# The second feed-forward of a two-layer block: another order of its seven-block products, and one low part moved from VectorE to GpSimd

## The chip, the core and the metric

The kernel runs on one core of a Trainium2 chip. The metric is device time in microseconds (us) of one execution, the median of several. The engines are named as in the profile: PE is TensorE (matmuls), PEld its weight loads, DVE is VectorE, ACT is ScalarE, POOL is GpSimd, SP is SyncE, which issues the DMAs here.

## What is computed

The program computes two model blocks of 1024 tokens by 1024 channels in float32. The change touches only the last stage, the feed-forward of the second block:

```python
h = rms_norm(x, norm_mlp[l])
x = x + jnp.square(jax.nn.relu(h @ w_up[l])) @ w_down[l]     # 1024 -> 4096 -> 1024
return rms_norm(x, norm_final)
```

## The kernel before

A float32 product is made of three matmuls of a faster format: every operand is split in a high part (a cast on ACT) and a low part (value minus high part), and the three are high by high, high by low and low by high. The `high` casts of weights are at L334 (ACT), the `low` subtractions of weights at L340 (POOL).

`square_ffn` cuts the 4096 hidden channels into 16 chunks of 256 (`chunks`). For a chunk the upward product (`up(i)`) and the downward product (`down(i)`) are each seen as a product of 2 by 2 blocks and made with seven block products instead of eight (the Strassen-Winograd scheme), named P1 to P7. The price is sums: of weight blocks (POOL, `pair_low` and `row_low`), of the activations' blocks (DVE, `first_blocks`, L2241 to L2246), of the upward results (DVE, `combine`, L2226 to L2235). Each of the seven products is 12 matmuls of 128x512, so a chunk is 168 matmuls. The program is pipelined by one chunk: `up(i)` and then `down(i)` run on PE, and `down(i)` takes the activations that `up(i - 1)` made. Chunk 16's rows of the downward product are done plainly at the end (`last_tile`), followed by the final norm. So PE does `up(0)`, `up(1)`, `down(1)`, then 14 times `up(i)`, `down(i)` for i = 2 to 15, then the last tiles.

The steps that the change touches:

- **The ring of weights** (`TurnRing`): a chunk has 14 split weight blocks, places 0 to 6 for `up`, 7 to 13 for `down`, in seven slots. A place can be written when the product seven places back has been taken (`used`). `split` counts finished low parts. The raw tiles (two, `core.raw`) hold by turns the chunk's two tiles of `w_up` and its two rows of `w_down`. `load_up` (SP) loads the next chunk's two `w_up` tiles once the low parts 12 and 13 are made. `weigh` (POOL, L396) multiplies each `w_up` tile by the norm's gain.
- **DVE's order in a chunk**: the low parts of the activation blocks P1, P2, P4 (`a_low`, L2220), sums, P5's low part, sums; `combine`; then `take` for the seven downward products in the order P1 P2 P5 P4 P6 P7 P3, with the low parts of P6, P7 and P3 between them. A `take` is four adds (L2256) of one PSUM bank each into X. PE writes the four banks in turn and needs a bank's add done before it writes that bank for the next product.
- **ACT's order in a chunk**, `fall(i - 1)` and then `rise(i)`:

```python
def fall(i, following):
    a_high(i, "P6")
    following(0)            # high(i + 1, 0): waits for weigh on POOL
    a_high(i, "P7")
    relu_first(i)
    a_high(i, "P3")
    following(1)
    relu_second(i)
    for n in range(2, 6):
        following(n)
```

`rise(i)` is `high(i, 6)`, `a_high(i, "P1", "P2", "P4", "P5")`, `keep(i)` (a copy of the first upward result, L2129, without which PE may not start the fifth upward product) and the seven casts of `w_down` blocks. Each engine works strictly in its written order; the waits are semaphores.
- **Start and end**: the second chunk's `w_up` tiles lie in a place of their own and POOL weighs them. Two differences in X (L2213, L2214) are made first of all on DVE, their sums (L2280, L2281) at the end, after the low parts of chunk 16 (L2278).

Of the kernel before, what the change touches and what calls it, by code (L numbers as in the profile page):

```python
# [23 lines left out]
P = 128  # L24
# [409 lines left out]
class TurnRing(Ring):  # L434


    UP, DOWN_PRODUCTS = 7, ("P1", "P2", "P5", "P4", "P6", "P7", "P3")
# [43 lines left out]
    def load_last(self, sp, i, sources):  # L481

        for n, p in enumerate((12, 13)):
# [20 lines left out]
    def row_low(self, pool, i):  # L504
# [11 lines left out]
        self.low(pool, i, 9, self.S)  # L516
        pool.wait_ge(self.split, self.done(i, 9))
# [451 lines left out]
class Program:  # L969
# [997 lines left out]
    def square_ffn(self, name, ring, W_up, W_down, rows):  # L1967
# [5 lines left out]
        MADE = ("P1", "P2", "P4", "P5", "P6", "P7", "P3")  # L1973
        PLACE = {"P1": 0, "P2": 1, "P4": 2, "P5": 3, "P6": 0, "P7": 1, "P3": 3}
        with ExitStack() as ctx:
# [6 lines left out]
                "kept", "u6", "u5", "u7", "c21", "c12", "relu", "sq", "a_sum", "a_hi", "a_lo", "down_mm", "down_add")}  # L1982
# [9 lines left out]
            ring.give_second([self.at(f"{name}_second_raw{k}", [P, UNIT], base + at * UNIT) for k, at in enumerate((8, 12))],  # L1992
# [20 lines left out]

            @block.sync
            def _(sp):
# [12 lines left out]
                sp.wait_ge(ring.used, ring.done(chunks - 1, 10))  # L2028
# [7 lines left out]
            def _(pool):  # L2036
# [16 lines left out]
            def _(pe):  # L2053
                def up(i):
                    X, Z, W, Y = up_banks(i)
                    out = {"P1": X, "P2": X, "P5": W, "P4": W, "P7": Z, "P3": Z, "P6": Y}
                    for n, product_name in enumerate(PRODUCTS):
                        more = product_name in ("P2", "P3", "P4")
                        if product_name == "P1" and not (isinstance(i, int) and i < 2):
                            pe.wait_ge(s["relu"], i * 3 - 2)  # L2060
                        elif product_name == "P5" and not (isinstance(i, int) and i < 2):
                            pe.wait_ge(s["relu"], i * 3 - 1)
# [18 lines left out]
                def down(i):  # L2081
                    for n, product_name in enumerate(DOWNS):
                        more = product_name in ("P2", "P3", "P4")
                        pe.wait_ge(ring.split, ring.done(i, 7 + n))
                        pe.wait_ge(s["a_lo"], made(i, MADE.index(product_name) + 1))
# [25 lines left out]
                pe.wait_ge(s["a_lo"], made(chunks, 2))  # L2111
# [6 lines left out]
            def _(act):  # L2118
# [12 lines left out]
                def relu_first(i):  # L2131
# [5 lines left out]
                    act.wait_ge(s["relu"], i * 3 + 1)  # L2137
                    act.activation(U[0], U[0], ACT.Square).then_inc(s["sq"], 1)

                def relu_second(i):  # L2140

                    if not (isinstance(i, int) and i == 0):
                        act.wait_ge(s["a_lo"], made(i, 7))
                    act.activation(A12, up_banks(i)[2], ACT.Relu).then_inc(s["relu"], 1)
                    act.activation(u22, u22, ACT.Relu).then_inc(s["relu"], 1)
                    act.wait_ge(s["relu"], i * 3 + 3)
                    act.activation(U[1], U[1], ACT.Square).then_inc(s["sq"], 1)

                def a_high(i, *names):

                    for x in names:
                        if x in ("P1", "P2", "P4"):
                            act.wait_ge(s["sq"], i * 2 - (1 if x == "P1" else 0))
                            if not (isinstance(i, int) and i == 1):
                                act.wait_ge(ring.used, ring.done(i - 1, 7 + DOWNS.index({"P1": "P6", "P2": "P7", "P4": "P4"}[x])))
                            else:
# [961 lines left out]
```

## Time and profile before

| | us |
|---|---|
| median of 3 runs | 2860.82 (2858.64 to 2862.8) |
| the profiled execution | 2861.63, its span 2859.9 |
| PE busy in the span | 2724.5 (95%) |
| DVE busy | 1750.1 (61%) |
| POOL busy | 1754.1 (61%) |
| ACT busy | 1129.4 (39%) |

The stage of the change is the last 680 us of the span. Busy shares are averages over all stages. A matmul's time in the rows is its own from start to end (about 0.39 us); since matmuls overlap, the distance between two starts is what one costs.

### The profile page before, as it was taken

What the parts mean: (1) busy time and instruction counts of PE and PEld (TensorE: products, weight loads), DVE (VectorE), ACT (ScalarE), POOL (GpSimd) and SP (SyncE); (2) the same over time, 40 slices, a digit from 0 to 9 for tenths busy, and PEclk for the clock granted to TensorE, in tenths of its full rate; (3) what the DMA queues carried; (4) which work ended last, traced back from release to release, by engine and by line L of the source; (5) the groups of instructions that cost most, each with busy time, mean ns of one, the idle gap of its engine ahead of it and who ended that gap; (6) DMA issues with size and microseconds to landing.
All of it is one profiled execution on the core that took longest, in us unless ns stands there. A gap on an engine that the chain in (4) does not pass through costs nothing. (4 is left out here: it accounts for less than half of the span.)

```text
span 2859.9 us, 39241 instructions
## 1 busy us (share of the span) xinstructions
PE 2724.5 (95%) x13371; PEld 2246.3 (79%) x13371; DVE 1750.1 (61%) x2209; ACT 1129.4 (39%) x1684; POOL 1754.1 (61%) x1201
## 2 busy tenths in 40 slices
PE   8999998999999999799999999999998999999998
PEld 7888886888888887678778878878786777777776
DVE  5334435565555656575685685685535877777778
ACT  4312316333332334555355345445333433443443
POOL 3323336767777676765565565565337787777782
PEclk9999999999999999899999999999999999999999
DMA  3111111111212113212111111112601111111112
GB/s 121 45 38 37 45 38 30 45 44 51 59 46 64 44 51 96 66 34 60 49 49 60 49 48 59 49 48 59 221 15 44 45 44 59 44 44 59 44 47 92
DMA packets 196117, 160.28 MB, mean 56 GB/s; under 512 B 5719, under 2 KB 176300, under 8 KB 196013
## 3 DMA queue, kind: packets, MB, share of 16 engines
q1 hardware_dynamic: 196013, 158.83, 18.1%
q8 instruction: 73, 1.20, 0.2%
q14 instruction: 31, 0.25, 0.0%
HBM read 143.08 MB, written 15.73 MB: 56 GB/s over the span
## 5 line engine op out<-in xcount | busy, mean ns | idle before, releaser
L340 POOL TENSOR_TENSOR w_lo<-w_raw,w_hi 128x512 fp32r<-128x512 f32 x336 | 466.2, 1395 | 316.9 <-ACT w_hi L334 316.9
L334 ACT CAST w_hi<-w_raw 128x512 fp32r<-128x512 f32 x336 | 202.8, 617 | 432.3 <-DMA w_raw<-in_w_in 106.2
L546 PE MATMUL PA<-h_hi,w_hi 128*128 128x512 f32 x636 | 260.7, 410 | 17.7 <-PEq L1035 5.6
L548 PE MATMUL PA<-h_hi,w_lo 128*128 128x512 f32 x636 | 250.0, 393 | 0.0
L547 PE MATMUL PA<-h_lo,w_hi 128*128 128x512 f32 x636 | 249.7, 393 | 0.0
L340 POOL TENSOR_TENSOR w_lo<-f_sums,w_hi 128x512 fp32r<-128x512 f32 x128 | 201.8, 1577 | 10.5 <-ACT w_hi L334 10.5
L396 POOL TENSOR_TENSOR w_raw<-w_raw,params 128x1024 f32<-128x1024 f32 x72 | 137.2, 1918 | 90.1 <-DMA w_raw<-in_w_up 45.5
L340 POOL TENSOR_TENSOR w_lo<-hy_ring_sums,w_hi 128x512 fp32r<-128x512 f32 x96 | 140.4, 1463 | 61.6 <-ACT w_hi L334 61.6
L546 PE MATMUL PB<-f_t_hi,w_hi 128*128 128x512 f32 x424 | 169.4, 400 | 8.5 <-ACT hy_tm L2797 5.0
L547 PE MATMUL PB<-f_t_lo,w_hi 128*128 128x512 f32 x424 | 166.3, 392 | 0.0
L548 PE MATMUL PB<-f_t_hi,w_lo 128*128 128x512 f32 x424 | 166.3, 392 | 0.0
L546 PEld LDWEIGHTS PA<-h_hi,w_hi 128*128 128x128 f32 x636 | 120.8, 190 | 47.8 <-issue 13.5
L2220 DVE TENSOR_TENSOR f_a_lo<-f_u,f_a_hi 128x512 fp32r<-128x512 f32 x105 | 122.4, 1188 | 58.1 <-ACT f_a_hi L2164 58.1
L125 POOL TENSOR_TENSOR w_hi<-w_raw,params 128x1024 fp32r<-128x1024 f32 x24 | 45.5, 1895 | 169.2 <-PE PB L136 82.8
L547 PEld LDWEIGHTS PA<-h_lo,w_hi 128*128 128x128 f32 x636 | 120.8, 190 | 27.3 <-issue 3.8
L548 PEld LDWEIGHTS PA<-h_hi,w_lo 128*128 128x128 f32 x636 | 120.5, 189 | 26.0
L2256 DVE TENSOR_TENSOR X<-X,MM 128x512 f32<-128x512 f32 x210 | 137.4, 680 | 0.2 <-PE MM L2093 0.2
L2256 DVE TENSOR_TENSOR X<-X,DD 128x512 f32<-128x512 f32 x210 | 136.8, 680 | 0.4 <-PE DD L2093 0.4
L409 POOL TENSOR_TENSOR hy_ring_sums<-w_raw 128x512 f32<-128x512 f32 x32 | 45.2, 1412 | 120.4 <-DMA w_raw<-in_w_in 120.4
L2091 PE MATMUL DD<-w_hi,f_a_hi 128*128 128x512 f32 x180 | 75.0, 416 | 43.6 <-DVE X L2256 43.6
L334 ACT CAST w_hi<-hy_ring_sums 128x512 fp32r<-128x512 f32 x96 | 59.6, 621 | 143.0 <-POOL hy_ring_sums L409 68.8
L334 ACT CAST w_hi<-f_sums 128x512 fp32r<-128x512 f32 x128 | 79.3, 619 | 79.5 <-POOL f_sums L421 35.8
(664 smaller groups left out, 8273.2 us busy)
## 6 DMA issues: line engine op xcount, KB each, us to landing
w_raw<-in_w_in SPq DMA_DIRECT2D x64, 512.0 KB, 5.2
w_raw<-in_ffn_w_up SPq DMA_DIRECT2D x42, 512.0 KB, 4.7
w_raw<-in_w_down SPq DMA_DIRECT2D x32, 512.0 KB, 3.7
w_raw<-in_w_up SPq DMA_DIRECT2D x30, 512.0 KB, 4.7
w_raw<-in_gla_w_in SPq DMA_DIRECT2D x24, 512.0 KB, 3.7
w_lo_raw<-in_ffn_w_down SPq DMA_DIRECT2D x44, 256.0 KB, 2.6
X<-in_x SPq DMA_DIRECT2D x8, 512.0 KB, 7.8
w_raw<-in_gla_w_out SPq DMA_DIRECT2D x8, 512.0 KB, 3.6
```

The lines of the kernel that those rows point to most:

```text
L125: pool.tensor_tensor(hi, raw, self.core.zero[:, 0:1].broadcast_to([P, UNIT]), ALU.add)\
L334: act.copy(self.slot(i, p)[0], source).then_inc(self.hi_done, 1)
L340: pool.tensor_tensor(lo, source, hi.bitcast(F32), ALU.subtract).then_inc(self.split, 1)
L396: pool.tensor_tensor(raw, raw, column.unsqueeze(2).broadcast_to([P, KT, P]), ALU.mult)\
L409: pool.tensor_tensor(self.S, a21, a22, ALU.add).then_inc(self.summed, 1)
L546: pe.matmul(bank, ah[:, k, :], bh[:, k, :], start=(k == 0 and not more), stop=False, skip_group_check=more)
L547: pe.matmul(bank, ah[:, k, :], bl[:, k, :], start=False, stop=False, skip_group_check=more)
L548: mm = pe.matmul(bank, al[:, k, :], bh[:, k, :], start=False, stop=(k == 3), skip_group_check=more)
L2091: pe.matmul(bank(b), hi[:, tok], wh, start=not more, stop=False, skip_group_check=more)
L2220: dve.tensor_tensor(alo[k], BLOCK[x], ahi[k].bitcast(F32), ALU.subtract).then_inc(s["a_lo"], 1)
L2256: dve.tensor_tensor(rows_, rows_, bank(b), op).then_inc(s["down_add"], 1)
```

## The change

Only the second feed-forward changes. The downward products run in the order P1 P2 P7 P3 P5 P4 P6 (before P1 P2 P5 P4 P6 P7 P3); the activation blocks are split in the order P4 P1 P2 P7 P3 P5 P6. The low part of P3's block is made by POOL, at the end of its chunk, and no longer by DVE. ACT casts all blocks before it starts the next chunk's weights; both relus of the second pair come before those of the first. The kept result lies in A21 and no longer in A22. The next chunk's `w_up` tiles are loaded after the low parts 9 and 12. ACT, not POOL, weighs the second chunk's tiles, with 16 multiplications of 128x128. The two differences in X come after `combine(0)`, and the low parts of chunk 16 before the last `take`.

```diff
-    UP, DOWN_PRODUCTS = 7, ("P1", "P2", "P5", "P4", "P6", "P7", "P3")
+    UP, DOWN_PRODUCTS = 7, ("P1", "P2", "P7", "P3", "P5", "P4", "P6")
@@ load_up, load_last
-        for n, p in enumerate((12, 13)):
+        for n, p in enumerate((9, 12)):
@@ row_low (POOL)
         pool.tensor_tensor(b12, b12, b22, ALU.subtract).then_inc(self.mixed, 1)
-        self.low(pool, i, 9, self.S)
-        pool.wait_ge(self.split, self.done(i, 9))
+        pool.wait_ge(self.mixed, first + 2)
+        self.low(pool, i, 9, b12)
+        self.low(pool, i, 10, b22)
+        self.low(pool, i, 11, self.S)
+        pool.wait_ge(self.split, self.done(i, 11))
         pool.tensor_tensor(self.S, b22, self.S, ALU.add).then_inc(self.mixed, 1)
         pool.wait_ge(self.mixed, first + 3)
         pool.tensor_tensor(b21, b21, self.S, ALU.subtract).then_inc(self.mixed, 1)
-        self.low(pool, i, 10, b21)
-        self.low(pool, i, 11, self.S)
-        self.low(pool, i, 12, b12)
-        self.low(pool, i, 13, b22)
+        pool.wait_ge(self.mixed, first + 4)
+        self.low(pool, i, 12, b21)
+        self.low(pool, i, 13, self.S)
@@ square_ffn
-        MADE = ("P1", "P2", "P4", "P5", "P6", "P7", "P3")
-        PLACE = {"P1": 0, "P2": 1, "P4": 2, "P5": 3, "P6": 0, "P7": 1, "P3": 3}
+        MADE = ("P4", "P1", "P2", "P7", "P3", "P5", "P6")
+        LATE = ('P3',)
+        EARLY = tuple(x for x in MADE if x not in LATE)
+        PLACE = {"P1": 0, "P4": 1, "P2": 2, "P7": 3, "P3": 0, "P5": 2, "P6": 3}
...
-            u22 = A22
+            u22 = A21
@@ POOL, chunk(i)
-                    ring.weigh(pool, i)
+                    if not (isinstance(i, int) and i == 1):
+                        ring.weigh(pool, i)
                     for part in range(2):
                         ring.pair_low(pool, i, 0, i, part)
                     ring.row_low(pool, i)
+                    for x in LATE:
+                        k = PLACE[x]
+                        pool.wait_ge(s["a_hi"], made(i, MADE.index(x) + 1))
+                        pool.tensor_tensor(alo[k], BLOCK[x], ahi[k].bitcast(F32), ALU.subtract)\
+                            .then_inc(s["a_lo_late"], 1)
@@ PE, up(i)
                         if product_name == "P1" and not (isinstance(i, int) and i < 2):
-                            pe.wait_ge(s["relu"], i * 3 - 2)
-                        elif product_name == "P5" and not (isinstance(i, int) and i < 2):
-                            pe.wait_ge(s["relu"], i * 3 - 1)
+                            pe.wait_ge(s["relu"], i * 3)
@@ ACT
                 def keep(i):
                     act.wait_ge(ring.used, ring.done(i, 0))
                     if not (isinstance(i, int) and i == 0):
-                        act.wait_ge(s["a_sum"], i * 4 - 1)
-                        act.wait_ge(s["a_lo"], made(i, 4))
+                        act.wait_ge(*low_done(i, "P7"))
...
+                def relu_second(i):
                     act.wait_ge(s["c12"], i + 1)
                     if not (isinstance(i, int) and i == 0):
-                        act.wait_ge(s["a_lo"], made(i, 6))
+                        act.wait_ge(*low_done(i, "P3"))
+                        act.wait_ge(*low_done(i, "P5"))
...
                 def rise(i):
+                    a_high(i, "P4", "P1", "P2")
                     high(i, 6)
-                    a_high(i, "P1", "P2", "P4", "P5")
+                    a_high(i, "P7")
                     keep(i)
...
                 def fall(i, following):
-                    a_high(i, "P6")
+                    a_high(i, "P3", "P5", "P6")
+                    relu_second(i)
                     following(0)
-                    a_high(i, "P7")
                     relu_first(i)
-                    a_high(i, "P3")
-                    following(1)
-                    relu_second(i)
-                    for n in range(2, 6):
+                    for n in range(1, 6):
                         following(n)
...
+                def weigh_second():
+                    for n in range(2):
+                        raw = ring.raw(1)[n].rearrange("p (k n) -> p k n", k=KT)
+                        act.wait_ge(*ring.arrived(n, 1))
+                        for k in range(KT):
+                            scaled = act.mul(raw[:, k, :], raw[:, k, :], c.par[:, ring.column + k:ring.column + k + 1])
+                        scaled.then_inc(ring.weighted, 1)
@@ ACT, the start
                 keep(0)
+                weigh_second()
                 high(0, 6)
-                high(1, 0, 1, 2, 3, 4)
+                high(1, 0, 1, 2, 3)
+                relu_second(0)
                 relu_first(0)
-                relu_second(0)
-                high(1, 5)
+                high(1, 4, 5)
                 rise(1)
@@ DVE
-                    for x in ("P1", "P2", "P4"):
+                    for x in ("P4", "P1", "P2"):
                         a_low(i, x)
                     dve.tensor_tensor(A22, A21, A22, ALU.add).then_inc(s["a_sum"], 1)
                     dve.tensor_tensor(A21, A11, A21, ALU.subtract).then_inc(s["a_sum"], 1)
-                    a_low(i, "P5")
+                    dve.wait_ge(s["a_sum"], i * 4 - 3)
                     dve.tensor_tensor(A11, A22, A11, ALU.subtract).then_inc(s["a_sum"], 1)
+                    a_low(i, "P7")
...
                     take(i, "P1")
                     take(i, "P2")
+                    a_low(i, "P5")
+                    take(i, "P7")
                     a_low(i, "P6")
+                    take(i, "P3")
                     take(i, "P5")
-                    a_low(i, "P7")
                     take(i, "P4")
-                    a_low(i, "P3")
+                    if isinstance(i, int) and i == chunks - 1:
+                        last_lows()
                     take(i, "P6")
-                    take(i, "P7")
-                    take(i, "P3")
...
                 combine(0)
+                dve.tensor_tensor(X12, X12, X22, ALU.subtract)
+                dve.tensor_tensor(X21, X21, X22, ALU.subtract)
                 chunk(1)
```

## Rows read from the trace of the kernel before

**Rows 1.** Busy time by stretch: chunk 1, and chunks 2 to 15

```profile
core 0: us, PE busy (x) PEld busy (x) DVE busy (x) ACT busy (x) POOL busy (x), PEclk, DMA share, GB/s
2180.50:2229.60 49.10, 40.62 (x168) 32.52 (x167) 30.20 (x44) 22.76 (x36) 38.35 (x30) 0.93 0.08 22
2229.60:2823.50 593.90, 552.45 (x2355) 448.83 (x2353) 457.58 (x618) 229.59 (x378) 453.75 (x331) 0.98 0.16 50
```

**Rows 2.** Waits from 2050 to 2860 us: total, times, longest

```profile
ACT w_hi L334 <- POOL w_raw L396: 94.6, 14, 7.2
...
PE DD L2091 <- DVE X L2256: 43.6, 22, 3.6
```

**Rows 3.** Timeline of PE: start, duration, work [idle before it, until whom]

```profile
2229.95 0.39 PE L2073 MATMUL PA<-h_hi,w_hi 128*128 128x512 f32 x1
...
2263.62 0.64 PE L2091 MATMUL DD<-w_hi,f_a_hi 128*128 128x512 f32 x1 [3.59 <-DVE X L2256]
2264.06 0.63 PE L2092 MATMUL DD<-w_lo,f_a_hi 128*128 128x512 f32 x1
...
2391.46 0.50 PE L2091 MATMUL DD<-w_hi,f_a_hi 128*128 128x512 f32 x1 [2.59 <-DVE X L2256]
2395.66 0.50 PE L2091 MATMUL DD<-w_hi,f_a_hi 128*128 128x512 f32 x1 [1.18 <-DVE X L2256]
...
2401.23 0.39 PE L2073 MATMUL PA<-h_hi,w_hi 128*128 128x512 f32 x1
...
2420.27 0.39 PE L2091 MATMUL DD<-w_hi,f_a_hi 128*128 128x512 f32 x1
...
2823.09 0.39 PE L2093 MATMUL MM<-f_seventh_hi,f_a_lo 128*128 128x512 f32 x1
```

**Rows 4.** Timeline of ACT in the chunk that starts at 2401.23

```profile
2402.42 1.66 ACT L2164 CAST f_a_hi<-f_u 128x512 fp32r<-128x512 f32 x3
...
2411.00 0.59 ACT L2129 COPY f_u<-PA 128x512 f32<-128x512 f32 x1 [1.44 <-DVE f_u L2244]
...
2430.93 0.62 ACT L334 CAST w_hi<-w_raw 128x512 fp32r<-128x512 f32 x1 [7.12 <-POOL w_raw L396]
```

**Rows 5.** Timeline of DVE around the same chunk

```profile
2393.50 1.51 DVE L2220 TENSOR_TENSOR f_a_lo<-f_u,f_a_hi 128x512 fp32r<-128x512 f32 x1 [0.30 <-ACT f_a_hi L2164]
...
2403.06 4.08 DVE L2220 TENSOR_TENSOR f_a_lo<-f_u,f_a_hi 128x512 fp32r<-128x512 f32 x3 [0.88 <-ACT f_a_hi L2164]
...
2426.52 0.69 DVE L2220 TENSOR_TENSOR f_a_lo<-f_u,f_a_hi 128x512 fp32r<-128x512 f32 x1
2427.12 1.28 DVE L2256 TENSOR_TENSOR X<-X,DD 128x512 f32<-128x512 f32 x2
2428.31 1.28 DVE L2256 TENSOR_TENSOR X<-X,MM 128x512 f32<-128x512 f32 x2
2432.10 1.40 DVE L2220 TENSOR_TENSOR f_a_lo<-f_u,f_a_hi 128x512 fp32r<-128x512 f32 x1 [2.51 <-ACT f_a_hi L2164]
```

**Rows 6.** Timeline of POOL in the same chunk

```profile
2404.25 1.74 POOL L340 TENSOR_TENSOR f_seventh_lo<-f_sums,f_seventh_hi 128x512 fp32r<-128x512 f32 x1
...
2412.19 2.56 POOL L340 TENSOR_TENSOR w_lo<-w_raw,w_hi 128x512 fp32r<-128x512 f32 x2 [3.90 <-ACT w_hi L334]
...
2420.78 1.30 POOL L340 TENSOR_TENSOR w_lo<-w_raw,w_hi 128x512 fp32r<-128x512 f32 x1 [0.80 <-ACT w_hi L334]
...
2424.55 1.29 POOL L340 TENSOR_TENSOR f_seventh_lo<-w_raw,f_seventh_hi 128x512 fp32r<-128x512 f32 x1
2428.92 1.91 POOL L396 TENSOR_TENSOR w_raw<-w_raw,params 128x1024 f32<-128x1024 f32 x1 [3.07 <-DMA w_raw<-in_w_up]
```

**Rows 7.** Timeline of PE in chunk 1 and at the end

```profile
2180.38 0.39 PE L2073 MATMUL PA<-h_hi,w_hi 128*128 128x512 f32 x1
...
2197.69 0.79 PE L2073 MATMUL PA<-h_hi,w_hi 128*128 128x512 f32 x1 [6.27 <-ACT f_u L2129]
...
2826.59 0.50 PE L134 MATMUL DD<-w_hi,h_hi 128*128 128x512 f32 x1 [3.11 <-DVE h_lo L2278]
```

More of the change, by code:

```diff
@@ L481, in load_last @@
     def load_last(self, sp, i, sources):
-        for n, p in enumerate((12, 13)):
+        for n, p in enumerate((9, 12)):
             sp.wait_ge(self.split, self.done(i - 1, p))
@@ L1981, in square_ffn @@
             s = {n: self.sem(f"{name}_{n}") for n in (
-                "kept", "u6", "u5", "u7", "c21", "c12", "relu", "sq", "a_sum", "a_hi", "a_lo", "down_mm", "down_add")}
+                "kept", "u6", "u5", "u7", "c21", "c12", "relu", "sq", "a_sum", "a_hi", "a_lo", "a_lo_late", "down_mm", "down_add")}
             adds = 28 * (chunks - 1)
@@ L2027, in _ @@
                 ring.load_last(sp, chunks, rows_of(chunks))
-                sp.wait_ge(ring.used, ring.done(chunks - 1, 10))
+                sp.wait_ge(ring.used, ring.done(chunks - 1, 11))
                 sp.dma_start(row, rows[0].partition_broadcast(P)).then_inc(fin.row_in, 16)
@@ L2084, in down @@
                         pe.wait_ge(ring.split, ring.done(i, 7 + n))
-                        pe.wait_ge(s["a_lo"], made(i, MADE.index(product_name) + 1))
+                        pe.wait_ge(*low_done(i, product_name))
                         hi, lo = ahi[PLACE[product_name]], alo[PLACE[product_name]]
@@ L2110, in _ @@
                     down(i)
-                pe.wait_ge(s["a_lo"], made(chunks, 2))
+                pe.wait_ge(s["a_lo"], len(EARLY) * (chunks - 1) + 2)
                 pe.wait_ge(ring.split, ring.done(chunks, 3))
@@ L2136, in relu_first @@
+                def relu_first(i):
+                    if not (isinstance(i, int) and i == 0):
+                        act.wait_ge(*low_done(i, "P6"))
                     act.activation(U[0], pair_of(i)[0], ACT.Relu).then_inc(s["relu"], 1)
-                    act.wait_ge(s["relu"], i * 3 + 1)
+                    act.wait_ge(s["relu"], i * 3 + 3)
                     act.activation(U[0], U[0], ACT.Square).then_inc(s["sq"], 1)
[L2140 to L2147, printed above, removed]
+                SLOT_BEFORE = {"P1": (1, "P3"), "P4": (1, "P4"), "P2": (1, "P5"), "P7": (1, "P6"),
+                               "P3": (0, "P1"), "P5": (0, "P2"), "P6": (0, "P7")}
@@ L2149, in a_high @@
+                SUM = {"P5": 1, "P7": 2, "P6": 3, "P3": 4}
                 def a_high(i, *names):
                     for x in names:
[L2152 to L2156, printed above, removed]
-                                act.wait_ge(ring.split, ring.done(1, 5))
-                        else:
-                            act.wait_ge(s["a_sum"], i * 4 - {"P5": 3, "P7": 2, "P6": 1, "P3": 0}[x])
-                            if x != "P5":
-                                act.wait_ge(ring.used, ring.done(i, 7 + DOWNS.index({"P6": "P1", "P7": "P2", "P3": "P5"}[x])))
-                            elif not (isinstance(i, int) and i == 1):
-                                act.wait_ge(ring.used, ring.done(i - 1, 13))
+                        if x in SUM:
+                            act.wait_ge(s["a_sum"], i * 4 - 4 + SUM[x])
+                        else:
+                            act.wait_ge(s["sq"], i * 2 - (0 if x == "P1" else 1))
+                        back, taker = SLOT_BEFORE[x]
+                        if not (isinstance(i, int) and i == 1 and back):
+                            act.wait_ge(ring.used, ring.done(i - back, 7 + DOWNS.index(taker)))
+                        elif x in ("P2", "P7"):
+                            act.wait_ge(ring.split, ring.done(1, 5 if x == "P2" else 4))
@@ L2256, in take, with last_lows @@
                         dve.tensor_tensor(rows_, rows_, bank(b), op).then_inc(s["down_add"], 1)
+                def last_lows():
+                    for k in (1, 0):
+                        dve.wait_ge(s["a_hi"], made(chunks, 2 - k))
+                        dve.tensor_tensor(last_lo[k], U[k], last_hi[k].bitcast(F32), ALU.subtract).then_inc(s["a_lo"], 1)
                 def chunk(i):
@@ L2262, in chunk @@
                     take(i, "P2")
+                    a_low(i, "P5")
+                    take(i, "P7")
                     a_low(i, "P6")
+                    take(i, "P3")
                     take(i, "P5")
-                    a_low(i, "P7")
                     take(i, "P4")
-                    a_low(i, "P3")
+                    if isinstance(i, int) and i == chunks - 1:
+                        last_lows()
                     take(i, "P6")
-                    take(i, "P7")
-                    take(i, "P3")
                 combine(0)
+                dve.tensor_tensor(X12, X12, X22, ALU.subtract)
+                dve.tensor_tensor(X21, X21, X22, ALU.subtract)
                 chunk(1)
-                with dve.Fori(2, chunks) as i:
+                with dve.Fori(2, chunks - 1) as i:
                     chunk(i)
-                for k in range(2):
-                    dve.wait_ge(s["a_hi"], made(chunks, k + 1))
-                    dve.tensor_tensor(last_lo[k], U[k], last_hi[k].bitcast(F32), ALU.subtract).then_inc(s["a_lo"], 1)
+                chunk(chunks - 1)
                 dve.wait_ge(s["down_add"], adds + 1)
```

17 lines of the change are left out of this document (11 added, 6 removed).

## The prediction

> **What bounds the kernel now.** I read the busy time by stretch first, then the waits, then the timelines of the four engines over one chunk. The page says that PE is busy 95% of the span, so only what PE waits for can be won. From the first matmul of `up(2)` at 2229.95 to the start of the last one of `down(15)` at 2823.09, 0.23 before its slot ends, PE takes 593.4 us for 14 chunks, 42.4 each [rows 3]. What a chunk would cost without waits comes from one upward half: 84 matmuls between 2401.23 and 2420.27, that is 19.04 us, or 0.227 a matmul [rows 3]; a chunk has 168, so 38.1. Each chunk loses 4.3 us.
>
> The waits say where: PE's four-bank products (L2091) stood 43.6 us behind DVE's adds into X [rows 2]. The timeline shows two forms. In one, PE waits 2.59 and, 4 us later, 1.18. In the other it waits once, up to 3.59, and the next matmuls then start 0.43 apart (2263.62, 2264.06) and not 0.23: the clock stands at its lower level for about nine of them, which costs 1.8 us [rows 3]. Both forms cost about 4.
>
> Why DVE is late is on its own timeline: after P5's take it stood idle 2.51 before P7's low part at 2432.10, until ACT's high part came [rows 5]. ACT had nothing to do for 7.12 until 2430.93, because the cast written ahead of P7's needs the next chunk's `w_up` tile weighed by POOL [rows 4]. That is the wait of 94.6 us over 14 chunks [rows 2]. POOL in turn waited 3.07 for a DMA that could start only when low part 12 was done (the low part 13 starts at 2424.55, the tile is there at 2428.92) [rows 6]. So the chain is DMA, weighing, ACT's order, DVE, PE. The second wait of 1.18 is a low part of 1.51 that DVE had to make when it was already as late as PE bears [rows 3, 5].
>
> **The change in a chunk.** Let t be the time since the first matmul of `up(i)`; the downward products start at 19.0, 21.8, 24.5, 27.2, 29.9, 32.6 and 35.4.
>
> *ACT's order.* `fall` now casts P3, P5 and P6 before anything that needs the next chunk. P5's slot is free at 24.5 (P2 done), its high part there at 25.1; DVE ends P2's take then too. P6's is there at 27.9, before DVE asks. The wait of 2.5 is gone. What takes its place: `following(0)` now stands behind `relu_second`, which needs P5's low part (26.6) and P3's from POOL, and `relu_first` behind P6's (about 30.5). With 2.1 for relu and square the relus end near 33; PE now wants all three before `up(i + 1)`, at 39. Six us of cover; nothing charged.
>
> *DVE between takes.* Three low parts become two. An add costs 0.60 when DVE runs behind (pairs at 2427.12 and 2428.31, 1.19 apart [rows 5]), PE makes a bank in 0.68, so DVE gains 0.32 a product, and it may be 3 x 0.68 - 0.60 = 1.4 late before PE stands. A low part is 0.69 when POOL is idle and 1.40 to 1.51 beside POOL's work [rows 5]; POOL will be at work, so I take 1.4. P5's uses the 1.4 up, P7's take gives 0.3 back, P6's 1.4 then costs PE 1.0. The trace's own price for this is 1.18 with a wait of 0.30 in it, 0.9 [rows 3, 5]. Bounds: 0.1 if both are quick, 1.7 if both last 1.74 like the slowed neighbour on POOL [rows 6]. The term is 1.0: a chunk of 39.1. One wait of this length left the matmul spacing at 0.23 (2395.66), so no clock is lost [rows 3].
>
> *DVE's first blocks.* They began at 2403.06, 0.88 late, for ACT's casts at 2402.42 stood behind a weight cast [rows 4, 5]. Those casts now come first. So P7's low part, and `keep` after it, come near t = 9.2 to 9.8 where `keep` was at 9.8 (2411.00) [rows 4]. PE needs it at 10.9: no wait, 0.5 to 1.1 of cover.
>
> *POOL.* It worked 453.75 / 14 = 32.4 us a chunk [rows 1]. P3's low part adds 1.3 (its 128x512 neighbours, 2.56 for two) to 1.74 [rows 6]; I take 1.4. Its new order also puts a wait for ACT's cast ahead of low part 9, as the one of 0.80 at 2420.78 [rows 6]. Walked: low part 7 starts 1.2 after `keep` starts (2412.19 after 2411.00), at 10.4 to 11.0; from there to the end of low part 13 it was 13.65 (2425.84), now 14.45; P3's ends 1.4 later, at t = 26.3 to 26.9 [rows 4, 6]. PE takes it at 27.2. The cover is thin, 0.3 to 0.9, and I charge nothing. All in all POOL has 32.4 + 1.4 + 0.8 for the new wait + 0.5 for more meetings with DVE = 35.1 of work and forced waiting, then the 0.8 that stays, 0.9 for the row DMA and about 1.3 between dependent sums: 38.1, one under PE's 39.1.
>
> *SP's queue.* The tiles are asked for after low parts 9 and 12, the second at t = 24, and need 4.4 (2428.92 less 2424.55) [rows 6], so 28.4; POOL has low part 13, P3's and the first weighing (1.91) until then. At most 0.5 idle, inside POOL's slack.
>
> **Chunk 1.** It lasts from 2180.38 to 2229.95, 49.6, 11.5 over the floor: PE waited 6.27 for `keep` and then ran at the lower clock [rows 3, 7]. POOL no longer weighs (2 x 1.91 [rows 6]). ACT does it in 16 pieces between two casts; for a 128x128 piece the trace has no row, and from its 128x512 casts of 0.62 [rows 4] each lies between a quarter, 0.16, and 0.62: 2.5 to 10 us, and I take 0.3 each, 4.8, which ends before POOL's next sum. But the two differences in X now lie on DVE ahead of the low parts, and P2's high part waits for a raw tile to be used up. I put `keep` 2.6 earlier, 2.5 more from a shorter spell of low clock and the downward waits: 5, bounds 0 (10 us of multiplications) and 8.
>
> **The end.** PE waited 3.11 for the low parts of chunk 16 and then lost about 1.8 in clock [rows 7]. They now lie before the last take, so PE stands about 1.2 there, and later about 1.5 because X's two sums keep DVE from the first adds. Saved: 4.9 - 2.7 = 2.2.
>
> **Sum.** 14 x (42.4 - 39.1) = 46, + 5 + 2 = 53. The profiled execution took 2861.6; 2861.6 - 53 = 2808.6. It lies 0.8 above the median of the runs, so 2808.
>
> The Trainium skill ("SBUF — State Buffer", "Who interferes with whom") says that a VectorE instruction with two SBUF inputs and a GpSimd instruction that reads SBUF exclude each other for the whole instruction, and "Perfetto Trace Analysis" ("Optimizing Scalar/DVE Operations") warns that moving work between the two might not help. The rows of 1.40 beside 0.69 agree, and the adds out of PSUM, at 1.28 a pair, show nothing of it. If every POOL operation and every such DVE operation of a chunk stood in one line, the result would be the third rival's.
>
> **The rivals.**
>
> *POOL sets the pace (24%).* If `keep` comes 1 us later or POOL's operations meet DVE more often, P3's low part ends after 27.2 and PE waits there, and DVE's lateness is partly made up meanwhile. For: cover of only 0.3 to 0.9. Against: POOL's own sum is 38.1. At 40.5 a chunk: 14 x 1.9 + 5 + 2 = 34 saved, 2827.
>
> *DVE's low parts stay hidden (14%).* One or both fall into POOL's idle time (0.69). Then 38.3 a chunk: 57 + 5 + 2 = 64, 2797.
>
> *The two engines exclude each other, and time is lost (9%).* This one ends on the other side. Its place is POOL's chain from low part 7 to P3's low part. It decides once that part ends after t = 27.2 + 4.3 + 0.5 = 32: from there the new wait of PE is longer than the old ones and the gain of start and end. For that each of POOL's 23 operations of 128x512 in a chunk must take 1.74 [rows 6] in place of 1.3, adding 10 us: 48 a chunk, 14 x 5.7 - 7 = 73 lost, 2934. Half of them would give 43, about the time before. Against it: beside DVE's three low parts in a row, 4.08 together, POOL lost only 0.45 once [rows 5, 6].
>
> *The reorder does nothing (3%),* because PE's wait has another releaser: 2861. The idle 2.51 and 7.12 speak against it.
>
> **How the numbers follow.** The forecast has 50%, its own range 2802 to 2817 (chunks of 38.7 to 39.7). The range of 2794 to 2833 takes in both neighbours and leaves out the last two. A measurement of this kernel can tell about 0.2% (6 us) from no change. Faster: 50 + 24 + 14 and a little of the third, 0.89; same 0.04; slower 0.07.
>
> **What would show it.** On the changed profile: a chunk of 39.1 on PE, with one wait of about 1.0 before the fifth downward product and none over 2; matmul spacing of 0.23 all through; ACT's `f_a_hi` waiting for PE and no longer behind `w_raw` L396; POOL's new low part on L340's sibling line at t = 26 to 27; PE's wait at 2197.69 shorter; no wait of 3.11 at the end. The prediction is wrong if PE waits before the fourth downward product (POOL), or before the fifth upward one (`keep`).

## The result

The changed kernel takes 2824.28 us (median of 4 runs, 2824.13 to 2824.3) against 2859.73 for the kernel before in the same session. The ratio is 0.9876 with a 95% interval of 0.9858 to 0.9893: 35.5 us won. The prediction was 2808 with a range of 2794 to 2833: the direction and the range held, the gain was forecast at 53, half as much again. The profiled execution has a span of 2822.4.

Busy time by stretch in the changed kernel, for chunk 1, chunks 2 to 15 and the end (the columns are those of [rows 1]):

```profile
2177.50:2225.00 47.50, 41.17 (x170) 33.01 (x169) 38.76 (x45) 23.22 (x37) 39.30 (x27) 0.93 0.08 23
2225.00:2788.00 563.00, 542.21 (x2353) 438.09 (x2351) 467.61 (x602) 229.78 (x375) 489.68 (x345) 1.00 0.18 53
2788.00:2822.40 34.40, 22.68 (x98) 17.86 (x96) 29.07 (x47) 10.06 (x24) 0.00 (x0) 0.91 0.31 123
```

From the first matmul of `up(2)` at 2224.90 to the end of `down(15)`'s last slot at 2788.19 the 14 chunks take 563.3 us, 40.2 each, where it was 42.4: 38.7 for the first and about 40.4 for those behind it. PE's granted clock is 1.00 in them, where it was 0.98. GpSimd works 35.0 us a chunk (489.68 / 14), where it was 32.4 [rows 1]. The timeline of PE shows the new waits of one chunk:

```profile
2424.88 0.39 PE L2107 MATMUL MM<-f_seventh_hi,f_a_lo 128*128 128x512 f32 x1
2425.11 0.39 PE L2087 MATMUL PA<-h_hi,w_hi 128*128 128x512 f32 x1
...
2437.42 0.49 PE L2087 MATMUL PA<-h_hi,w_hi 128*128 128x512 f32 x1 [1.27 <-ACT f_u L2142]
...
2454.31 0.49 PE L2105 MATMUL DD<-w_hi,f_a_hi 128*128 128x512 f32 x1 [0.29 <-DVE X L2278]
```

The waits of 2.59 and 1.18 [rows 3] are gone. In their place PE waits 1.3 before the fifth upward product, for ACT's copy (`keep`), and 0.3 before the fourth downward one, P3's (three products of 2.72 after 2445.70). From start to start these cost about 1.5 and 0.7 in the chunk shown, which takes 40.3; over the 14 chunks, of which the first has neither, it is about 1.5 and 0.6, and with 38.1 that is the 40.2. The second wait is named after DVE's add, but that add had ended at about 2453.5, as the pair that began at 2452.84 shows, and GpSimd's low part of P3 only at 2454.0:

```profile
2452.84 1.27 DVE L2278 TENSOR_TENSOR X<-X,DD 128x512 f32<-128x512 f32 x2
```

```profile
2452.33 1.74 POOL L2059 TENSOR_TENSOR f_a_lo<-f_u,f_a_hi 128x512 fp32r<-128x512 f32 x1
2454.03 4.21 POOL L396 TENSOR_TENSOR w_raw<-w_raw,params 128x1024 f32<-128x1024 f32 x2
```

In the run below without that low part this wait is absent. Why the copy is late is on DVE and ACT. DVE's first blocks, then ACT's casts ahead of them:

```profile
2424.63 1.37 DVE L2278 TENSOR_TENSOR X<-X,MM 128x512 f32<-128x512 f32 x2
2426.82 4.14 DVE L2241 TENSOR_TENSOR f_a_lo<-f_u,f_a_hi 128x512 fp32r<-128x512 f32 x3 [0.83 <-ACT f_a_hi L2179]
2430.89 1.78 DVE L2262 TENSOR_TENSOR f_u<-f_u,f_u 128x512 f32<-128x512 f32 x1
2432.59 1.77 DVE L2263 TENSOR_TENSOR f_u<-f_u 128x512 f32<-128x512 f32 x1
2434.28 1.79 DVE L2265 TENSOR_TENSOR f_u<-f_u,f_u 128x512 f32<-128x512 f32 x1
2436.00 0.68 DVE L2241 TENSOR_TENSOR f_a_lo<-f_u,f_a_hi 128x512 fp32r<-128x512 f32 x1
```

```profile
2424.61 0.62 ACT L334 CAST w_hi<-f_sums 128x512 fp32r<-128x512 f32 x1 [2.00 <-POOL f_sums L421]
2425.14 1.14 ACT L334 CAST w_hi<-w_raw 128x512 fp32r<-128x512 f32 x2
2426.18 1.66 ACT L2179 CAST f_a_hi<-f_u 128x512 fp32r<-128x512 f32 x3
...
2436.71 0.58 ACT L2142 COPY f_u<-PA 128x512 f32<-128x512 f32 x1 [1.62 <-DVE f_a_lo L2241]
```

Two things are to be seen. DVE's three sums take 1.78 each; in the trace of before one of them did and two took 0.68. (The third takes 1.78 in 7 of the 14 chunks; in the chunk before this one it took 0.68, and P7's low part behind it 1.54 in its place.) And DVE still stands 0.83 before its first low part, because the casts of the activation blocks are written behind three weight casts, of which the first waits for GpSimd's third sum. The copy of the chunk before is on ACT at 2396.34:

```profile
2396.34 0.58 ACT L2142 COPY f_u<-PA 128x512 f32<-128x512 f32 x1 [1.60 <-DVE f_a_lo L2241]
```

The timeline of POOL from there on shows that it now works beside DVE's second and third sum (2432.08 and 2434.24), where it had stood idle for 3.90 [rows 6]:

```profile
2397.52 2.55 POOL L340 TENSOR_TENSOR w_lo<-w_raw,w_hi 128x512 fp32r<-128x512 f32 x2 [1.76 <-ACT w_hi L334]
...
2411.96 1.76 POOL L2059 TENSOR_TENSOR f_a_lo<-f_u,f_a_hi 128x512 fp32r<-128x512 f32 x1
2413.68 4.21 POOL L396 TENSOR_TENSOR w_raw<-w_raw,params 128x1024 f32<-128x1024 f32 x2
2418.07 1.30 POOL L409 TENSOR_TENSOR f_sums<-w_raw 128x512 f32<-128x512 f32 x1 [0.18 <-POOL w_raw L396]
...
2423.21 1.29 POOL L421 TENSOR_TENSOR f_sums<-f_sums,w_raw 128x512 f32<-128x512 f32 x1
...
2428.68 3.43 POOL L340 TENSOR_TENSOR w_lo<-w_raw,w_hi 128x512 fp32r<-128x512 f32 x2
2432.08 1.73 POOL L340 TENSOR_TENSOR f_seventh_lo<-f_sums,f_seventh_hi 128x512 fp32r<-128x512 f32 x1
2434.24 1.29 POOL L510 TENSOR_TENSOR f_sums<-w_raw 128x512 f32<-128x512 f32 x1 [0.43 <-DMA w_raw<-in_w_down]
```

Read from one copy (2396.34) to the next (2436.71), the chain closes on itself: 1.2 to low part 7, 14.4 to P3's low part (2411.96), 1.7 for it, 4.4 for the two weighings, 6.4 to the end of the third sum, 2.3 through ACT's casts, 4.1 for three low parts on DVE, 5.1 for its three sums, 0.7 for P7's low part: 40.4. This loop is longer than PE's 38.1, so PE waits in every chunk but the first. The theory that the runs led to is this loop (L), with the meetings of DVE and GpSimd in it (M: the two make each other's operations longer). The rivals were that the meetings alone count, that GpSimd's chain alone is the pace (P), and that ACT's order alone was the whole gain. The expectations of the first four runs go by M and its rivals; L was put on record only after them.

### The profile page after: what moved, and what is told of

Same layout as the page of the kernel before. It is cut to its first block and busy times, and to the rows that moved or that the text cites. A ratio compares the mean times of both kernels' runs of the same rounds, so it can differ in the third digit from the quotient of the medians.

```text
span 2822.4 us, 39258 instructions
## 1 busy us (share of the span) xinstructions
PE 2713.2 (96%) x13371; PEld 2235.3 (79%) x13371; DVE 1765.8 (63%) x2194; ACT 1136.1 (40%) x1700; POOL 1785.2 (63%) x1214
## 5 line engine op out<-in xcount | busy, mean ns | idle before, releaser
L340 POOL TENSOR_TENSOR w_lo<-w_raw,w_hi 128x512 fp32r<-128x512 f32 x351 | 495.3, 1420 | 293.9 <-ACT w_hi L334 293.9
L334 ACT CAST w_hi<-w_raw 128x512 fp32r<-128x512 f32 x351 | 209.7, 617 | 388.8 <-DMA w_raw<-in_w_in 121.2
L340 POOL TENSOR_TENSOR w_lo<-f_sums,w_hi 128x512 fp32r<-128x512 f32 x113 | 174.0, 1540 | 10.7 <-ACT w_hi L334 10.7
L548 PEld LDWEIGHTS PA<-h_hi,w_hi 128*128 128x128 f32 x636 | 120.9, 190 | 47.9 <-issue 13.7
L409 POOL TENSOR_TENSOR hy_ring_sums<-w_raw 128x512 f32<-128x512 f32 x32 | 44.3, 1385 | 121.5 <-DMA w_raw<-in_w_in 121.5
L2241 DVE TENSOR_TENSOR f_a_lo<-f_u,f_a_hi 128x512 fp32r<-128x512 f32 x90 | 110.6, 1254 | 12.9 <-ACT f_a_hi L2179 12.9
L334 ACT CAST w_hi<-hy_ring_sums 128x512 fp32r<-128x512 f32 x96 | 59.6, 621 | 139.5 <-POOL hy_ring_sums L409 68.2
L334 ACT CAST w_hi<-f_sums 128x512 fp32r<-128x512 f32 x113 | 70.2, 621 | 111.8 <-POOL f_sums L421 60.9
L2179 ACT CAST f_a_hi<-f_u 128x512 fp32r<-128x512 f32 x105 | 62.2, 619 | 119.5 <-DVE f_u L2263 74.7
```

The lines of the kernel that those rows point to most:

```text
L334: act.copy(self.slot(i, p)[0], source).then_inc(self.hi_done, 1)
L340: pool.tensor_tensor(lo, source, hi.bitcast(F32), ALU.subtract).then_inc(self.split, 1)
L409: pool.tensor_tensor(self.S, a21, a22, ALU.add).then_inc(self.summed, 1)
L548: pe.matmul(bank, ah[:, k, :], bh[:, k, :], start=(k == 0 and not more), stop=False, skip_group_check=more)
L2179: act.copy(ahi[PLACE[x]], BLOCK[x]).then_inc(s["a_hi"], 1)
L2241: dve.tensor_tensor(alo[k], BLOCK[x], ahi[k].bitcast(F32), ALU.subtract).then_inc(s["a_lo"], 1)
```

## The experiments

Twelve kernels in three groups, each beside the kernel before on the same chip (2859.84, 2860.82 and 2858.53). The changed kernel itself was not run again beside them. Its median of 2824.28, to which some differences below are taken, is from the session of the result, and what a kernel saved against its own kernel before can give a difference up to 1.2 us smaller or larger.

**One line of ACT in the kernel before.**

```diff
                     a_high(i, "P6")
-                    following(0)
                     a_high(i, "P7")
+                    following(0)
```

> The kernel before, with one line moved on ACT: the cast of P7's block ahead of the next chunk's first weight cast. If the wait of 2.5 us for that cast was the main loss and nothing follows it up, 14 x 2.5 = 35 is saved, 2825, as much as the whole change. If DVE's three low parts between the takes then cost PE by themselves (1.0 to 1.2 each after the first), it is 42.4 - 2.5 + 1.0 = 40.9 a chunk, 2839. If the chain of the kernel before is another one, nothing moves, 2860.

2856.27, ratio 0.9987 [0.9977, 0.9996]: 3.6 us, between 1.1 and 6.6 by the interval. DVE's wait of 2.5 for P7's block went. PE still waits at two takes, 1.0 and 0.8, and a new wait of 1.6 came at the copy. The timeline of PE in two neighbouring chunks:

```profile
2407.57 0.49 PE L2073 MATMUL PA<-h_hi,w_hi 128*128 128x512 f32 x1 [1.59 <-ACT f_u L2129]
2427.92 0.50 PE L2091 MATMUL DD<-w_hi,f_a_hi 128*128 128x512 f32 x1 [1.02 <-DVE X L2256]
2431.70 0.50 PE L2091 MATMUL DD<-w_hi,f_a_hi 128*128 128x512 f32 x1 [0.79 <-DVE X L2256]
2449.90 0.49 PE L2073 MATMUL PA<-h_hi,w_hi 128*128 128x512 f32 x1 [1.54 <-ACT f_u L2129]
```

A chunk is 42.3 (2449.90 less 2407.57), as before. DVE is on time at the takes and then stands still for its first low part, as its timeline shows:

```profile
2441.25 4.07 DVE L2220 TENSOR_TENSOR f_a_lo<-f_u,f_a_hi 128x512 fp32r<-128x512 f32 x3 [3.03 <-ACT f_a_hi L2164]
```

```profile
2440.07 0.62 ACT L334 CAST f_seventh_hi<-f_sums 128x512 fp32r<-128x512 f32 x1 [2.21 <-POOL f_sums L426]
2440.60 1.66 ACT L2164 CAST f_a_hi<-f_u 128x512 fp32r<-128x512 f32 x3
```

ACT casts the activation blocks right behind the seventh weight cast, which waits for GpSimd's last sum. The timeline of POOL has one more piece, the wait for the next chunk's tile:

```profile
2424.82 4.21 POOL L396 TENSOR_TENSOR w_raw<-w_raw,params 128x1024 f32<-128x1024 f32 x2 [3.12 <-DMA w_raw<-in_w_up]
```

From one copy (2406.86) to the next (2449.18) it closes: 1.2 to low part 7, 13.7 to the end of low part 13, 3.1 for the tile, 4.4 for the weighings, 10.7 to the end of the fourth sum, 1.3 through ACT, 4.0 for three low parts on DVE, 3.9 to the copy: 42.3. The visible wait of the kernel before was therefore not its price: the chain over GpSimd, the DMA, ACT, DVE, the copy and GpSimd again stood behind it and kept the chunk at 42.3. The kernel before shows the same link, DVE's wait of 0.88 for the casts behind the seventh weight cast [rows 5]. The expectations of 2825 and 2839 took the visible wait for its price. The third, another chain and 2860, was right in kind, and nearly in time. Only one cast of ACT's new order was moved here, not all of it.

**P3's low part back on DVE.**

```diff
-        LATE = ('P3',)
+        LATE = ()
...
                     take(i, "P1")
+                    a_low(i, "P3")
                     take(i, "P2")
```

> The changed kernel, with the low part of P3 back on DVE, between the takes of P1 and P2. Theory M (meetings): the changed kernel's wait of 1.5 us a chunk before the fifth upward product comes from DVE's three sums of activation blocks, 1.78 each instead of 0.68 because GpSimd now works beside them. GpSimd's work shrinks by 1.76 a chunk here, so it is done a little earlier before the sums, and DVE has one more low part between the takes, which costs PE about 1.0: 2815 to 2835, the wait at the copy smaller, the wait at the takes larger. Rival P (GpSimd's chain is the real pace): a chunk gets 1.8 shorter, 2799.

2830.92, ratio 0.99 [0.9883, 0.9916], 6.6 us behind the changed kernel's median, as M had it. The wait at the copy is gone, the second sum (L2263) has a median of 679 ns, and in most chunks PE waits three times at the takes:

```profile
2454.27 0.50 PE L2105 MATMUL DD<-w_hi,f_a_hi 128*128 128x512 f32 x1 [0.34 <-DVE X L2278]
2457.83 0.50 PE L2105 MATMUL DD<-w_hi,f_a_hi 128*128 128x512 f32 x1 [0.54 <-DVE X L2278]
2461.93 0.50 PE L2105 MATMUL DD<-w_hi,f_a_hi 128*128 128x512 f32 x1 [1.09 <-DVE X L2278]
```

So with the rest of the change in place the one low part on GpSimd is worth about 7 of the 35.5 us. What the others are worth is not split by this run.

**GpSimd held back while DVE sums.**

```diff
                     ring.low(pool, i, 4, ring.block("P2", i))
+                    if not (isinstance(i, int) and i == 1):
+                        pool.wait_ge(s["a_sum"], i * 4 - 1)
                     ring.low(pool, i, 5, ring.block("P4", i))
```

> The changed kernel, with GpSimd held back ahead of low part 5 until DVE has made its third sum, in chunks 2 to 15. Theory M: the three sums take 0.68 each, the copy comes 3 us earlier, PE's wait of 1.5 before the fifth upward product goes, and GpSimd's loss of about 2.5 is covered since it stands idle later in the chunk anyhow: 2803 to 2812. Rival Q (the copy is late because ACT's casts start DVE's first low parts late): no change, 2824. Rival P (GpSimd's chain is the pace): 14 x 2.5 = 35 slower, 2859.

2826.83, ratio 0.9884 [0.9868, 0.9901]. The mechanism is as M says: DVE's sums are short.

```profile
2434.04 0.68 DVE L2267 TENSOR_TENSOR f_u<-f_u,f_u 128x512 f32<-128x512 f32 x1
2434.64 0.68 DVE L2268 TENSOR_TENSOR f_u<-f_u 128x512 f32<-128x512 f32 x1
2435.24 0.68 DVE L2270 TENSOR_TENSOR f_u<-f_u,f_u 128x512 f32<-128x512 f32 x1
...
2454.71 1.58 DVE L2246 TENSOR_TENSOR f_a_lo<-f_u,f_a_hi 128x512 fp32r<-128x512 f32 x1 [1.09 <-ACT f_a_hi L2184]
```

PE's wait at the copy is gone too. But GpSimd is 2.5 us later, ACT casts P5's block behind GpSimd's last sums, DVE's low part of P5 comes 1.09 late (last row), and P3's low part on GpSimd ends at 2457.4; PE, which waited 2.04 before its product, goes on at 2457.65. In three of the 14 chunks PE's granted clock then fell to 0.50 (from 2498.49 on, nine matmuls 0.43 apart), so a part of this time is the clock's. The gain was lost again because GpSimd had no such time to spare, against my expectation. P's 2859 was wrong as well: the loop gained 3.3 on DVE and lost 2.5 on GpSimd.

**DVE's third sum behind P7's low part.** The copy overwrites A21 and has to wait for P7's low part, not for the sum in A11.

```diff
-                    for x in ("P4", "P1", "P2"):
-                        a_low(i, x)
+                    a_low(i, "P4")
                     dve.tensor_tensor(A22, A21, A22, ALU.add).then_inc(s["a_sum"], 1)
                     dve.tensor_tensor(A21, A11, A21, ALU.subtract).then_inc(s["a_sum"], 1)
+                    a_low(i, "P1")
+                    a_low(i, "P2")
+                    a_low(i, "P7")
                     dve.wait_ge(s["a_sum"], i * 4 - 3)
                     dve.tensor_tensor(A11, A22, A11, ALU.subtract).then_inc(s["a_sum"], 1)
-                    a_low(i, "P7")
```

> The changed kernel, with another order on DVE: low part P4, the first two sums, low parts P1, P2, P7, and only then the third sum, which the copy does not need. GpSimd has the same work. Theory M: the copy comes 1.8 to 2 us earlier and PE's wait of 1.5 before the fifth upward product goes; 38.7 to 39.2 a chunk, 2803 to 2810. Rival P (GpSimd's chain is the pace): unchanged, 2824.

2816.74, ratio 0.9854 [0.9837, 0.987]: 7.5 us better than the changed kernel, where 14 to 21 were expected. The wait at the copy is gone with GpSimd's work unchanged, which P alone cannot explain. What is left is one wait at the takes, before the fifth downward product: 39.8 a chunk. DVE's two low parts there are now 1.36 and 1.86, and P3's on GpSimd is done in time.

```profile
2415.64 0.50 PE L2105 MATMUL DD<-w_hi,f_a_hi 128*128 128x512 f32 x1 [1.13 <-DVE X L2279]
2455.45 0.50 PE L2105 MATMUL DD<-w_hi,f_a_hi 128*128 128x512 f32 x1 [1.11 <-DVE X L2279]
```

**The loop, shortened and lengthened.** In the first kernel P3's low part is left out (the product takes an older one); in the second the tiles are asked for as before.

```diff
-                        pool.tensor_tensor(alo[k], BLOCK[x], ahi[k].bitcast(F32), ALU.subtract)\
-                            .then_inc(s["a_lo_late"], 1)
+                        pool.sem_inc(s["a_lo_late"], 1)
```

> The changed kernel without P3's low part on GpSimd: it is left out and nothing makes it (the product takes an older low part), only the count is raised. Theory L (a loop): GpSimd's chain from low part 7 to its third sum, ACT's casts behind that sum, DVE's low parts and sums and the copy form one loop of 40.3 us, longer than PE's 38.1. It gets 1.76 shorter: 38.6 a chunk, 2800 to 2806. Theory M alone (only the meetings of DVE and GpSimd count, GpSimd has time to spare): the sums still last 1.78 each, 2818 to 2824.

```diff
@@ load_up, load_last
-        for n, p in enumerate((9, 12)):
+        for n, p in enumerate((12, 13)):
```

> The changed kernel with the next chunk's tiles asked for after low parts 12 and 13 again, not 9 and 12. GpSimd then waits for the second tile about 0.5 to 1.5 us longer after the first weighing; theory L has that in the loop: 14 x 0.5 to 1.5 = 7 to 21 slower, 2831 to 2845. If GpSimd had time to spare: 2824.

Without the low part: 2815.2, 39.8 a chunk, with the wait at the copy (1.3) as the only one. Neither figure was met, and the timeline of POOL says why the loop lost 0.6 and not 1.76: the second tile's DMA, asked for at low part 12, is now the later one.

```profile
2446.49 1.30 POOL L340 TENSOR_TENSOR f_seventh_lo<-f_sums,f_seventh_hi 128x512 fp32r<-128x512 f32 x1
2447.75 2.35 POOL L396 TENSOR_TENSOR w_raw<-w_raw,params 128x1024 f32<-128x1024 f32 x1
2450.67 2.42 POOL L396 TENSOR_TENSOR w_raw<-w_raw,params 128x1024 f32<-128x1024 f32 x1 [0.57 <-DMA w_raw<-in_w_up]
2453.27 1.30 POOL L409 TENSOR_TENSOR f_sums<-w_raw 128x512 f32<-128x512 f32 x1 [0.18 <-POOL w_raw L396]
```

From the end of low part 13 to the start of the first sum of weights (L409) it is 5.5 where 1.7 + 4.4 was. With the old loads: 2841.43, 17 us slower than the changed kernel, within what L gave and against a GpSimd with time to spare. Its timeline has the cause. GpSimd stands idle 1.3 to 1.9 before each first weighing, most often 1.4, and the 14 chunks take 41.7 each where the loop of the changed kernel has 40.4. One of the longer waits:

```profile
2418.34 4.21 POOL L396 TENSOR_TENSOR w_raw<-w_raw,params 128x1024 f32<-128x1024 f32 x2 [1.90 <-DMA w_raw<-in_w_up]
```

So nearly half of the whole gain hangs on asking for the tiles earlier: 16 us by what each kernel saved against its own kernel before, 17 by the medians. The prediction had given this edit no gain.

**Both orders together.** The third sum moved and P3's low part on DVE, the two edits shown above.

> Both orders: DVE's third sum behind P7's low part, as in the run with that order alone (2816.7), and P3's low part on DVE. Theory L: the loop is short on both counts and the takes alone set the pace; DVE has three low parts there, 40.9 a chunk as in the run with only P3 on DVE: 2829 to 2833. If the loop still counted there, the shorter order would give something: 2815 to 2824.

2817.43, ratio 0.9849 [0.9832, 0.9865], as with the sum moved and P3's low part on GpSimd: with that order, moving the low part is worth nothing. The three low parts between the takes are 0.80, 1.25 and 1.52 in one chunk, 3.6 together where two were 3.2. GpSimd's waits for ACT's casts are 77.4 us in the 14 chunks against 57.3 with P3's low part on GpSimd. The expectation of L, 2829 to 2833, was wrong: the price at the takes is not a fixed one per low part; that it hangs on what GpSimd does at that moment fits these durations, but no run here varied that alone.

**The place of the low parts between the takes.** All three have the third sum moved. The first has P6's low part one take later, the second P5's on GpSimd in place of P3's, the third both.

```diff
                     take(i, "P7")
-                    a_low(i, "P6")
                     take(i, "P3")
+                    a_low(i, "P6")
...
                     following(0)
+                    following(1)
                     relu_first(i)
-                    for n in range(1, 6):
+                    for n in range(2, 6):
```

```diff
-        LATE = ('P3',)
+        LATE = ('P5',)
...
                     take(i, "P1")
+                    a_low(i, "P3")
                     take(i, "P2")
-                    a_low(i, "P5")
```

> The order of the best run so far (third sum behind P7's low part, 2816.7, 39.8 a chunk), and DVE's low part of P6 one take later, behind P3's; on ACT the second weight cast of the next chunk comes ahead of the first relu pair. In that run the wait of PE is only at the takes, 1.7 a chunk, after two low parts of 1.36 and 1.86 with one take between them. DVE wins 0.3 a take, so with two takes between: 39.4 to 39.5 a chunk, 2811 to 2813. If the GpSimd-ACT-DVE loop (38.7 by the trace's pieces) is in truth the pace there: 2817 or later, since a relu comes later.

> The order of the best run so far, with P5's low part on GpSimd in place of P3's; DVE makes P3's low part behind the first take. The work of both engines is the same. DVE's two low parts have two takes between them: 39.4 a chunk, 2811. GpSimd has 2.7 us more until PE wants its low part. If only the amount of work on each engine counts, not its place: 2817.

> Both edits of the two runs beside it: P3's low part behind the first take, P6's behind the fourth, P5's on GpSimd. Three takes between the two low parts give back 0.9 to 1.0: 39.1 a chunk, 2807 to 2809, if the takes are the pace. The loop of 38.7 is then near; if it takes over, 2809 to 2817.

2812.06 (0.9833 [0.9816, 0.9849]), 2817.37 and 2813.14. The first met its figure: 39.4 a chunk, 12 us better than the changed kernel, and with the third the fastest here. It did not meet it by the way that was expected, a smaller wait at the takes as the pace. The wait of 1.1 before the fifth downward product is gone, and in most chunks PE waits at a take only briefly and before the sixth upward product:

```profile
2447.52 0.50 PE L2105 MATMUL DD<-w_hi,f_a_hi 128*128 128x512 f32 x1 [0.16 <-DVE X L2280]
2472.87 0.49 PE L2087 MATMUL PB<-f_t_hi,w_hi 128*128 128x512 f32 x1 [0.38 <-DVE f_u L2250]
```

The second won nothing, since P6's low part lay beside the weighings (GpSimd was at them from 2448.91 to 2452.7) and took 2.06 from 2451.16 on. The third is no better than the first: in both, the chain through DVE's first blocks is back as the bound, now one product later, where PE waits for `combine`. The waits of the third, at a take and at the sixth upward product:

```profile
2444.57 0.50 PE L2105 MATMUL DD<-w_hi,f_a_hi 128*128 128x512 f32 x1 [0.42 <-DVE X L2280]
2472.42 0.49 PE L2087 MATMUL PB<-f_t_hi,w_hi 128*128 128x512 f32 x1 [0.30 <-DVE f_u L2250]
```

**The start.** The differences in X ahead of all again; and the second chunk's tiles weighed by GpSimd again.

```diff
                 dve.sem_inc(s["down_add"], 1)
+                dve.tensor_tensor(X12, X12, X22, ALU.subtract)
+                dve.tensor_tensor(X21, X21, X22, ALU.subtract)
...
                 combine(0)
-                dve.tensor_tensor(X12, X12, X22, ALU.subtract)
-                dve.tensor_tensor(X21, X21, X22, ALU.subtract)
```

> The changed kernel with the two differences in X ahead of everything on DVE again. In the kernel before they lay beside GpSimd's first two operations, which took 3.3 each instead of 1.3. If that is what made the first upward product 2.1 us longer before, 2826 to 2828, with less wait at the copy in chunk 1 perhaps taking 1 to 2 of it back. If the 2.1 have another source: 2824 or less.

```diff
-                    if not (isinstance(i, int) and i == 1):
-                        ring.weigh(pool, i)
+                    ring.weigh(pool, i)
...
-                weigh_second()
```

> The changed kernel with the second chunk's tiles weighed by GpSimd again, not by ACT. GpSimd's chain in chunk 1 is 3.8 us longer and the copy 3 to 4 us later, in that chunk only: 2827 to 2828. If chunk 1 has cover, 2824.

2824.58 and 2826.94, ratios 0.9871 [0.9855, 0.9888] and 0.9886 [0.9869, 0.9902]; both intervals hold the changed kernel's 0.9876. In the first, GpSimd's first operations are slow again (3.33 and 3.21), and the fifth upward product of chunk 1 starts 38.4 after the stage's first, 36.7 in the changed kernel. The time does not show the 1.6, and the trace says where it went: chunk 1 then takes 45.5 where it took 47.4, so `up(2)` starts 68.4 after the stage's first matmul, 68.2 in the changed kernel. In the second the copy's wait in chunk 1 is 7.83 where it was 4.92, and `up(4)` starts 149.7 after the stage's first matmul, 147.2 in the changed kernel. The medians, 0.3 and 2.7 apart, fit these 0.2 and 2.5 but would not show them alone.

## Why the prediction was right in direction and too high in gain

- **What bounded the kernel before.** The waits were read rightly, the price was not: the single ACT line that removes the wait of 2.5 is worth 3.6 us in all. Behind it stood a loop of 42.3 through GpSimd and back. I took the chain for a line (DMA, weighing, ACT, DVE, PE) and did not follow it from DVE's first blocks on to the copy and to GpSimd again.
- **ACT's order.** Right: no cast of P5 or P6 waits for weights any more, and the relus had cover.
- **DVE between takes.** Mis-sized: nothing instead of 1.0. The low parts took 0.92 and 1.25 instead of 1.4 each, by the prediction's own sum 0.4 for PE, and PE's short wait for GpSimd leaves DVE time to make that up; no run separates the two. The sum itself holds where both are long: for 1.36 and 1.86 it gives 1.5, and PE lost 1.7 in that run.
- **DVE's first blocks: the step that failed.** It had the copy at t = 9.2 to 9.8, before PE's 10.9. It starts at 11.6 (2436.71 less 2425.11), and PE loses 1.5 instead of nothing. With the 0.6 for P3's low part in place of the 1.0 at the takes, that makes 1.1 a chunk, 14 x 1.1 = 15 of the 17.5 us missed. Two parts of it were wrong. "Those casts now come first" is so for the seventh weight cast only; three others, one behind GpSimd's third sum, stay ahead, and DVE stood 0.83 where 0 was assumed. And two of the three sums (or one of them and P7's low part) cost about 1.1 more each because GpSimd no longer stands idle beside them; with GpSimd held back they took 0.68. I had put "0.5 for more meetings" on GpSimd and nothing on DVE.
- **GpSimd.** From low part 7's start to P3's low part 14.45 was forecast and 14.4 measured. But P3's was done at t = 28.9 (2454.03 less 2425.11), since its start hangs on the copy, and not at 26.3 to 26.9, and the product waited 0.6 for it. The sum of 38.1 was no bound by itself, but its pieces stand in the loop of 40.4.
- **SP's queue.** Given no gain, it is worth 16 to 17 us once the loop is the pace. That the range held is in part luck: the prediction counted on GpSimd's slack and not on this edit, and without it the kernel takes 2841, outside the range. The forecast's own range of 2802 to 2817 did not hold; the wide one did because it took in the neighbour on GpSimd.
- **Chunk 1 and the end.** Chunk 1 went from 49.6 to 47.4, 2.2 for a forecast 5: PE still waited 4.92 and the lower clock came after it. The 16 multiplications took 4.79, as estimated. The end gave 2.4 for a forecast 2.2. The first upward product's 2.1, for the differences in X moved away from GpSimd's start, was not forecast, and by the run with these two ahead again it is no gain of its own: chunk 1 would have been 1.9 shorter with them. With 0.8 of the stages ahead, 30.1 + 2.2 + 2.4 + 2.1 + 0.8 make up the 37.5 between the two spans.
- **The rivals.** "POOL sets the pace" came true in size (40.5 a chunk, 2827), and for a third in its place: 0.6 of the 2.1 is the wait for P3's low part, 1.5 the one for the copy. Its condition, a copy 1 us later and more meetings, was what happened. The rule of the Trainium skill on the two engines ("SBUF — State Buffer", "Who interferes with whom") is borne out where operations meet: DVE's two-input sums take 1.78 beside a busy GpSimd and 0.68 when it is held back, and the adds out of PSUM stay at 1.27 a pair. The time of the third rival, 48 a chunk, did not come: a chunk took 40.4.

## What to carry to other kernels

A wait that ends last need not be worth its length: follow the chain on past the waiting engine until it either ends or comes back to where it began, and price the loop, for an iteration cannot be shorter than that. Removing idle time on GpSimd made DVE's SBUF-to-SBUF sums beside it longer (0.68 to 1.78), so price those at their contended duration as soon as the plan fills the gaps. When a loop of 40 us runs over four engines, the order of operations that the next engine does not need (here one sum, 7.5 us) is worth as much as moving work (one low part, 6.6 us). And an edit that only asks for data earlier (here 16 us) is worth nothing or much by whether the loop runs through it.

## What the runs showed of the hardware that was not expected

The meetings are lopsided: DVE's 128x512 sum goes from 0.68 to 1.78, GpSimd's low part from 1.3 to 1.7 (two of them 3.43). With 128x2048 differences on DVE (the run with them ahead of all) it is GpSimd that suffers: 3.33 for an operation of 1.29, while DVE's takes 3.32 instead of 2.29. In the changed kernel the first of them started 0.2 before a sum of GpSimd and kept its 2.29, and the second, already behind that sum, took 3.38:

```profile
2178.28 2.29 DVE L2302 TENSOR_TENSOR X<-X 128x2048 f32<-128x2048 f32 x1
2180.49 3.38 DVE L2303 TENSOR_TENSOR X<-X 128x2048 f32<-128x2048 f32 x1
```

```profile
2178.49 3.23 POOL L426 TENSOR_TENSOR f_sums<-f_sums,f_second_raw 128x512 f32<-128x512 f32 x1
```

From the end of DVE's first difference (2180.57) GpSimd's sum needs 1.15 more, and from the end of that sum (2181.72) DVE's second difference needs 2.15: each about its own time alone. So these rows fit the two taking turns by whole operations. The sums of the chunk come near to it as well: by the rows, one of each takes 1.70 from start to start, where alone they take 0.60 and 1.25. The one with the short operations then loses most. No run varied the lengths to test this.
